# Start of a two-layer decoder trunk: loads on another queue, turns in another order, first matmul chunk in three parts, zero fills later

## The reference

```python
for i in range(2):
    x = x + 0.5 * swiglu(rmsnorm(x, ffn1_norm[i]), ffn1_w_in[i], ffn1_w_out[i])    # hidden 2816
    x = x + (s5_mixer, hgrn2_mixer)[i](rmsnorm(x, mix_norm[i]), ...)
    x = x + cross_attend(rmsnorm(x, xattn_norm[i]), mem_k[i], mem_v[i], w_q, w_o)  # 256 memory tokens
    x = x + 0.5 * swiglu(rmsnorm(x, ffn2_norm[i]), ffn2_w_in[i], ffn2_w_out[i])
y = rmsnorm(x, final_norm)
# s5: 64 groups of 16 channels, each with a 64-dim complex diagonal state
#   lam_bar = exp(lam * dt); b_bar = (lam_bar - 1) / lam * b; h_t = lam_bar * h_(t-1) + b_bar u_t
#   y_t = Re(c h_t) + d u_t, then gelu and a gated linear unit
```

## Time and profile before

| | |
|---|---|
| median of 3 runs | 2545.82 us (2538.57 to 2549.84) |
| the profiled execution | 2546.63 us |
| its span | 2544.9 us |
| PE, DVE, ACT, POOL busy | 97%, 49%, 34%, 24% of the span |
| mean granted PE clock | 0.985 |
| DMA | 289.16 MB, mean 114 GB/s |

### The profile page before, as it was taken

The page is one execution under the profiler, slowest core; times in us unless marked ns, Lnnn a source line. Parts: engine busy times, 40 slices in busy tenths (PEclk is TensorE's granted clock), DMA queues, the critical chain, the costliest instruction groups (busy, mean ns, idle before and its releaser), DMA issues.

```text
span 2544.9 us, 49720 instructions
## 1 busy us (share of the span) xinstructions
PE 2462.6 (97%) x21037; PEld 2370.9 (93%) x21037; DVE 1258.5 (49%) x1764; ACT 853.5 (34%) x1228; POOL 612.7 (24%) x604
## 2 busy tenths in 40 slices
PE   6999999799999999999999999999998999999999
PEld 6999999688976999999999999999998959999998
DVE  4553543854555543344543244466776565442443
ACT  3332221443222322222333133266664233221222
POOL 5579948241201100001211010331122203000003
PEclk8999999899999999999999999999999999999999
DMA  8255444363354333233443333333332543332332
GB/s 163 84 165 128 123 123 147 104 201 107 110 196 133 91 91 105 79 90 100 143 117 114 99 92 107 92 86 101 94 103 63 200 158 89 93 101 86 90 99 76
DMA packets 479670, 289.16 MB, mean 114 GB/s; under 512 B 22352, under 2 KB 467024, under 8 KB 478480
## 3 DMA queue, kind: packets, MB, share of 16 engines
q1 hardware_dynamic: 473760, 280.66, 37.6%
q0 software_dynamic: 848, 1.89, 0.7%
q10 hardware_dynamic: 4896, 4.20, 0.5%
HBM read 258.86 MB, written 27.85 MB: 113 GB/s over the span
## 4 chain that ended last, share of the span: by engine, by line
PE 91%; DVE 4%; ACT 2%; DMA 1%; issue 1%; POOL 1%; SPq 0%; DVEq 0%; ACTq 0%; POOLq 0%
PE lin L2670 76%; PE mis L2237 3%; DMA raw<-in_ffn_w_in_dram 1%; PE mis L2358 1%; DVE w_lo L1668 1%; DVE rstd L1681 1%; PE mis L2343 1%; PE mis L2293 1%; PE lin L2358 1%; PE mis L2523 1%; PE mis L2515 0%; PE lin L2601 0%; POOL w_lo L975 0%; DVE a_lo L1674 0%; DVE kc L1726 0%
## 5 line engine op out<-in xcount | busy, mean ns | idle before, releaser
L2670 PE MATMUL lin<-a_hi,w_hi 128*128 128x260 f32 x3584 | 1023.9, 286 | 18.9 <-DVE w_lo L1668 15.0
L2670 PE MATMUL lin<-a_lo,w_hi 128*128 128x260 f32 x3584 | 1015.8, 283 | 0.0
L2670 PE MATMUL lin<-a_hi,w_lo 128*128 128x260 f32 x3584 | 1015.2, 283 | 0.0
L2670 PEld LDWEIGHTS lin<-a_hi,w_hi 128*128 128x128 f32 x3584 | 677.1, 189 | 25.6 <-issue 12.8
L1668 DVE TENSOR_TENSOR w_lo<-raw,w_hi 128x1024 fp32r<-128x1024 f32 (+1 forms) x328 | 499.1, 1522 | 403.8 <-ACT w_hi L1239 403.4
L2670 PEld LDWEIGHTS lin<-a_hi,w_lo 128*128 128x128 f32 x3584 | 678.2, 189 | 0.0
L2670 PEld LDWEIGHTS lin<-a_lo,w_hi 128*128 128x128 f32 x3584 | 677.9, 189 | 0.2
L2670 PE MATMUL lin<-h_hi,w_hi 128*128 128x260 f32 x2016 | 570.1, 283 | 4.6 <-DVE h_lo L1898 1.7
L2670 PE MATMUL lin<-h_hi,w_lo 128*128 128x260 f32 x2016 | 569.3, 282 | 0.0
L2670 PE MATMUL lin<-h_lo,w_hi 128*128 128x260 f32 x2016 | 568.5, 282 | 0.0
L1239 ACT ACTIVATE w_hi<-raw 128x1024 fp32r<-128x1024 f32 (+1 forms) x328 | 364.5, 1111 | 320.1 <-PE lin L2670 300.0
(11 more groups left out here) (453 smaller groups left out, 2586.9 us busy)
## 6 DMA issues: line engine op xcount, KB each, us to landing
raw<-in_ffn_w_in_dram SPq DMA_DIRECT2D x176, 512.0 KB, 3.8
raw<-in_ffn_w_out_dram SPq DMA_DIRECT2D x64, 704.0 KB, 4.6
kc<-in_cache_mem_k_dram SPq DMA_DIRECT2D x32, 512.0 KB, 5.3
vc<-in_cache_mem_v_dram SPq DMA_DIRECT2D x16, 1024.0 KB, 8.6
raw<-in_hg_w_in_dram SPq DMA_DIRECT2D x32, 512.0 KB, 4.1
raw<-in_xattn_w_kv_dram SPq DMA_DIRECT2D x16, 512.0 KB, 4.3
raw<-in_s_w_glu_dram SPq DMA_DIRECT2D x16, 512.0 KB, 4.0
raw<-in_xattn_w_q_dram SPq DMA_DIRECT2D x16, 512.0 KB, 4.0
```

The source lines that it names most:

```text
L2670: ins = pe.matmul(lin[:, j, half, 0:HT], w[:, j, k, :], x[:, k, cols], start=k == 0 and u == 0, stop=k == kt - 1 and u == 2)
```

## The change

1. The nine `vrows` loads are issued by ACT, ahead of everything else it does; the memset of `vrows` is gone, and PE turns 113 rows instead of 128.
2. PE turns the prompt first, `vrows` behind it, the sample rows last. DVE copies in the same order.
3. ACT's first weight split stands behind two `a_hi` tiles instead of ahead of all.
4. The first chunk runs in three parts: all `w_hi*a_hi`, all `w_lo*a_hi`, all `w_hi*a_lo`, each waiting only for what it reads.
5. `cRaw` is loaded behind the weight loads of pair 1, `bRaw` behind those of pairs 3 and 4. The semaphore they shared is two.
6. The zero fills stand on POOL behind the state-space parameters and ahead of the wait for `mem_out`.

```diff
+            def s5_matrices(i):
+                if i == 1:
+                    for q, name in enumerate(("s5_c_re", "s5_c_im")):
+                        for e in range(2):
+                            sp.dma_start(cRaw[:, q, :, 64 * e:64 * e + 64],
+                                         i_[name][0].rearrange("(t g) c p -> (g c) t p", t=8)).then_inc(s5_cin, 16)
+                else:
+                    q = i - 3
+                    b = i_[("s5_b_re", "s5_b_im")[q]][0].rearrange("(j g) p c -> g p j c", g=2)
                     for g in range(2):
-                        sp.dma_start(bRaw[64 * g:64 * g + 64, q], b[g]).then_inc(s5_bc, 16)
...
+                        if ST[n][:2] == ("ffn1_in0", 0) and (i, j) in ((1, 1), (3, 1), (4, 1)) and s5_norm is not None:
+                            s5_matrices(i)
@@ POOL
-            step.link(pool.memset(vrows[:], 0.0))
-            for name, row in (("ffn1_norm", V_FFN1), ...):
-                pool.dma_start(vrows[row:row + 2 * KD, :], ...).then_inc(vrows_loaded, 16)
...
-            pool.wait_ge(consts_done, 4)
-            for d in range(CS - 1):
-                n = SC * (CS - 1 - d)
-                pool.dma_start(s5_t[SC * d:SC * (d + 1), :, 0:n],
-                               zeros[0:SC, 0:n].unsqueeze(1).to_broadcast([SC, SG, n]))\
-                    .then_inc(s5_zeros_out, 16)
...
                 pool.wait_ge(s5p_fill, S5P.at("c", (1, 1)) + 1)
+                pool.wait_ge(consts_done, 4)
+                for d in range(CS - 1):
+                    n = SC * (CS - 1 - d)
+                    pool.dma_start(s5_t[SC * d:SC * (d + 1), :, 0:n],
+                                   zeros[0:SC, 0:n].unsqueeze(1).to_broadcast([SC, SG, n]))\
+                        .then_inc(s5_zeros_out, 16)
                 pool.wait_ge(mem_out, 16 * 2 * DEPTH)
@@ ACT
+            for name, row in (("ffn1_norm", V_FFN1), ...):
+                act.dma_start(vrows[row:row + 2 * KD, :], ...).then_inc(vrows_loaded, 16)
...
-            split(0, 0, ST[0][3])
...
             for m in range(KD):
+                if m == 2:
+                    split(0, 0, ST[0][3])
                 gain_hi(m, NORM_ROW[0])
@@ PE
-            pe.wait_ge(vrows_loaded, 16 * 9)
-            pe.transpose(lin[:, 0, 0, 0:P], vrows[:], ident[:]).then_inc(vec_tr, 1)
             for t in range(4):
                 pe.wait_ge(rows_in[t], 16)
...
+            pe.wait_ge(vrows_loaded, 16 * 9)
+            pe.transpose(lin[:, 0, 0, 0:NVEC], vrows[0:NVEC, :], ident[0:NVEC, 0:NVEC]).then_inc(vec_tr, 1)
...
+                def first_chunk():
+                    pe.wait_ge(hi_ready, 1)
+                    for u, (w, x) in enumerate(((w_hi, x_hi), (w_lo, x_hi), (w_hi, x_lo))):
+                        if u == 1:
+                            pe.wait_ge(lo_ready, 1)
+                        for k in range(kt):
+                            if u == 0:
+                                pe.wait_ge(a_hi_done, k + 1)
+                            if u == 2:
+                                pe.wait_ge(a_lo_done, k + 1)
+                            for half in range(2):
+                                ins = pe.matmul(lin[:, 0, half, 0:HT], w[:, 0, k, :], x[:, k, half * HT:(half + 1) * HT],
+                                                start=k == 0 and u == 0, stop=k == kt - 1 and u == 2)
+                    ins.then_inc(chunk_done, 1)
+                    first_sums()
```

More of the change, by code:

```diff
@@ L372, in trunk_kernel @@
     gated = sem("gated")
-    s5_rows, s5_bc, s5_small = sem("s5_rows"), sem("s5_bc"), sem("s5_small")
+    s5_rows, s5_bin, s5_cin, s5_small = sem("s5_rows"), sem("s5_bin"), sem("s5_cin"), sem("s5_small")
     s5_sin, s5_phase, s5_square, s5_inverse = sem("s5_sin"), sem("s5_phase"), sem("s5_square"), sem("s5_inverse")
@@ L705, in s5_parameters @@
                 sp.dma_start(ldrow[64:96, :], i_["s5_log_dt"][0].rearrange("(j g) -> j g", g=2)).then_inc(s5_rows, 16)
-                for q, name in enumerate(("s5_b_re", "s5_b_im")):
-                    b = i_[name][0].rearrange("(j g) p c -> g p j c", g=2)
-                    for g in range(2):
-                        sp.dma_start(bRaw[64 * g:64 * g + 64, q], b[g]).then_inc(s5_bc, 16)
[L710 to L713, removed]
+            def s5_matrices(i):
[7 more added lines that the diff above has]
+                    b = i_[("s5_b_re", "s5_b_im")[q]][0].rearrange("(j g) p c -> g p j c", g=2)
+                    for g in range(2):
+                        sp.dma_start(bRaw[64 * g:64 * g + 64, q], b[g]).then_inc(s5_bin, 16)
             def kv_memory(l):
@@ L1083, in s5_discretize @@
                 powers(pool, link, pw, bTmp)
-                pool.wait_ge(s5_bc, 16 * 8)
+                pool.wait_ge(s5_bin, 16 * 4)
                 col = [v[q].unsqueeze(2).to_broadcast([P, NJ, SC]) for q in (6, 7)]
@@ L1249, in gain_hi @@
                                scale=vec[:, bass.ds(row + m, 1)]).then_inc(a_hi_done, 1)
+            for name, row in (("ffn1_norm", V_FFN1), ("mix_norm", V_MIX), ("xattn_norm", V_XA), ("mem_norm", V_MEM),
+                              ("ffn2_norm", V_FFN2), ("hg_lb_logits", V_LB)):
+                act.dma_start(vrows[row:row + 2 * KD, :], i_[name].rearrange("l (k p) -> (l k) p", p=P))\
+                    .then_inc(vrows_loaded, 16)
+            act.dma_start(vrows[V_FIN:V_FIN + KD, :], i_["final_norm"].rearrange("(k p) -> k p", p=P))\
+                .then_inc(vrows_loaded, 16)
+            act.dma_start(vrows[V_D:V_D + KD, :], i_["s5_d"][0].rearrange("(k g) c -> k (g c)", k=KD))\
+                .then_inc(vrows_loaded, 16)
+            act.dma_start(vrows[V_HG:V_HG + 1, :], i_["hg_norm"]).then_inc(vrows_loaded, 16)
             for t in range(4):
@@ L1681, in reciprocal @@
                 step.link(dve.reciprocal(rstd[:], t1[:]))
-            dve.wait_ge(vec_tr, 1)
-            dve.tensor_copy(vec[:], lin[:, 0, 0, 0:NVEC]).then_inc(vec_done, 1)
             for t in range(4):
@@ L1689, in _ @@
                                 mis[:, 2 * t % 4, :].rearrange("p (k t) -> p k t", k=4)).then_inc(in_evac["dve"], 1)
+            dve.wait_ge(vec_tr, 1)
+            dve.tensor_copy(vec[:], lin[:, 0, 0, 0:NVEC]).then_inc(vec_done, 1)
             dve.wait_ge(in_tr, 9)
@@ L2276, in prepare @@
                     elif what == "c":
-                        pe.wait_ge(s5_bc, 16 * 8)
+                        pe.wait_ge(s5_cin, 16 * 4)
                         e, f = a
@@ L2658, in stream @@
                     x_done, x0 = a_lo_done, KD * split_norms.index(r_in)
+                def first_chunk():
[13 more added lines that the diff above has]
+                    first_sums()
                 def chunk(p, j, first):
+                    if first and r == 0:
+                        first_chunk()
+                        return
                     pe.wait_ge(lo_ready, 2 * p + j + 1)
@@ L2672, in chunk @@
                     ins.then_inc(chunk_done, 1)
-                    if first and r == 0:
-                        first_sums()
-                    elif first and r is not None:
+                    if first and r is not None:
                         sums(r)
```

## The result

| | before | after |
|---|---|---|
| median of 20 runs each, in turn on one chip | 2545.81 us (2537.94 to 2551.33) | 2551.94 us (2544.05 to 2680.72) |
| ratio of after to before, 95% | | 1.0023 (1.0013 to 1.0033) |
| the profiled execution, its span | 2546.63, 2544.9 us | 2558.74, 2556.9 us |
| mean granted PE clock | 0.985 | 0.981 |

One run of after, that of 2680.72 us, had a granted clock of 0.85 where the others have 0.98, and the ratio leaves it out. The ratio is 5.9 us, between 3.3 and 8.4; the forecast was +3.6. So the kernel is slower, by less than the 0.5% that the prediction set as its bound. The profiled execution of after lies 6.8 us above its median (it is the slowest of the other nineteen), that of before 0.8; its stretches show where time goes, and the ratios how much it is in all.

A forecast was written before the change was run, and what follows sets the result against it. PE, busy 97% of the span, was taken as the bound. On the profiled 2546.6 us, -11.4 for the start and +15.0 for the fills gave 2550.2, forecast as 2550 us; whole range 2534 to 2559, the forecast's own 2545 to 2556.

The forecast's parts named there:

- Turns, issue of `vrows`, split: At the start: turns follow the landings, last tile done at 11.2 us; `a_hi` starts at 12.6, 7.0 us earlier.
- First chunk: At the start: only two `w_hi*a_lo` matmuls stand behind the last `a_lo`; it ends at 25.8 us, 11.7 us gained.
- Clock: At the first sums and second chunk: PE's clock may fall after idling, losing 0 to 4.2 us; taken as 1.
- Start in all: The start, with the stop at pair 1: 11.7 - 1.0 + 0.7 = 11.4 us gained, between 8 and 12.4.
- Fills, step 1: At the fills' new place on POOL: issued from 148.3 us, they fill the engines 23.9 us, until 172.2.
- stretched: Rival at the new place: fills and traffic slow each other, fills last 30 us; loss 24, time 2558 us; chance 0.09.
- Steps 2 and 3: Behind the fills: the load of chunk (10,1) takes 19 us instead of 3.8, and PE stands still 9.5 us.
- Step 4: At `ffn1_out0`: its load lands at 181.8 us; PE begins at 185.6 instead of 170.6, 15.0 us lost in all.
- Step 5: At POOL's tables: they start 16 us late and would hold PE 12.6 us, less than the 15 already lost.
- hidden: Rival at the new place: weight loads pass the fills, or fills end sooner; 2534 us, or 2533; chance 0.16.
- half: Rival at the new place: the load of chunk (10,1) takes some 12 us, not 19; 2541 to 2543 us; chance 0.15.
- The start does not follow: Rival at the start: clock stays down through the sums, or turns wait; 4 us less gain, 2554 us; no chance given.

The follow-up runs named there:

- experiment 11: The kernel before with only the zero fills spread over POOL's later tables: median 2543.51 us, ratio to before 0.9984.
- experiment 2: The kernel before with only the zero fills moved to the new place, ahead of the wait for `mem_out`: median 2560.05 us, ratio to before 1.0069.
- experiment 7: The changed kernel with the fills on ACT's hardware queue, behind the split of chunk (9,1) and ahead of the load of (10,1): one run, 2556.89 us.
- experiment 1: The changed kernel with the zero fills back in their old place behind POOL's squares: median 2538.24 us, ratio to before 0.9981.
- experiment 10: The changed kernel with fills spread over POOL's later tables, and the `vrows` loads back on POOL's queue: median 2533.93 us, ratio to before 0.9944.
- experiment 3: The changed kernel with the zero fills spread over POOL's later state-space tables: median 2531.42 us, ratio to before 0.9955.
- experiment 8: The changed kernel with fills spread over POOL's later tables, and the first chunk back in its old order: median 2537.02 us, ratio to before 0.9955.

## Why the prediction was right, and which terms were off

The forecast of 2550 us, +0.2%, holds, and its mechanism with it. By its own steps, in the profiled execution:

- **Turns, issue of `vrows`, split.** Turns began at 4.34 us (forecast 4.3). The nine issues held ACT until 5.1 us (4.2), and its first copy began at 6.40; `vrows` had landed when PE wanted it. The last tile was turned at 12.46, not 11.2. The forecast took 1.3 us a tile from the 5.12 us of the earlier trace rows, but that is a mean of two paces: 12 of those turns took 2.77 us, the other 20 only 2.35. In the profiled execution of after all 32 ran at the slow pace, 1.84 us a tile, so that the third tile, started at 8.78, still held PE when the fourth had landed (at about 10.1, forecast 9.9). That is the 1.0 us by which `a_hi` is late. The granted clock reads 1.00 in both stretches, so no row says why the pace differs. In the eight other runs with the new start and `vrows` on ACT the pace rose earlier, and PE came to `vrows` at 9.61 to 11.13 us (forecast 11.2).
- **First chunk.** Ended at 27.4 us (25.8). DVE's string took 12.2 us (12.0), and with the 1.0 us it ended 1.1 late; the last matmuls behind it ran at the lower clock (0.50 in the window from 26 us).
- **Clock.** Taken as 1 us: the sums took 4.76 instead of 3.67, so it was right in after; in the run with spread fills the window from 26 to 30 us was at 1.00, and nothing was lost. Both were within the bounds. The sums lost 1.1 to 1.7 us in three of the ten profiled executions with the new start, and nothing in seven.
- **Pair 1.** The stop of 0.7 us is gone, as forecast. By experiment 11 the early fills cost more than their stop, 4.1 us (1.3 to 7.1); the forecast had nothing for that.
- **Start in all.** 10.2 us against 11.4, bounds 8 to 12.4. Together with spread fills it is worth 11.4 us by the ratio, alone 7.4 by ratios and 11.7 by marks (experiment 11).
- **Matrices.** Nothing, as forecast, and the run with them in their old place agrees.
- **Fills, step 1.** Forecast to last 23.9 us; they lasted 28, most of the way to the 30 of the "stretched" rival. In the old place they took 24.1 us. Whether the traffic of q1 stretches them is open: beside the same loads and stores they took 25.4 us in experiment 2. The 0.36 us a packet of the prediction mixes the 288 packets of `vrows` in; the 560 of the fills, 73.9% of the engines from 29 to 54 us before, are 0.53 us each. The forecast of 23.9 us did not rest on it.
- **Steps 2 and 3.** The load took 20.6 us (19), the first stop was 11.0 (9.5).
- **Step 4.** The second load landed at 173.8 us. The forecast, 181.8, is 171.6 in these times. `ffn1_out0` began 6.9 us later than before; with the 10.2 of the start, 17.1 us were lost there, against 15.0.
- **What the step left out.** I had counted the lower clock after the stop for chunk (10,1), where the second stop hides it, but not after the second stop: from 177.41 to the mark are 10.7 us, before 8.1. That is 2.6 us more. It stood only in the "stretched" rival.
- **Step 5.** POOL's tables were 18 us late in shifted times (16), and PE did not wait for them. The run with the parking stores moved shows how near they were.

So the term that was mis-sized is the cost of the fills: 15.0 us forecast, 19.7 by the trace of after, 17.6 (13.5 to 21.4) with the fills moved alone, 17.3 (12 to 22) between after and spread fills. The start was 1.2 us too high. Both errors have the same sign, so they did not cancel; the sum came out as +3.6 against +5.9 (3.3 to 8.4). The prediction also held that a change under 0.5% could not be told from none. With 20 runs each, 0.23% could: the interval does not reach 1.

The rivals: "hidden" and "half" are out, by the 20.6 us of the load. "Stretched" was right that PE meets `ffn1_out0` at the lower clock; its 30 us of fills were not reached (28.0), and the weight load had landed 3.3 us before the last fill. "The start does not follow" is out.

The place of the fills was the whole question, and a rule of the Trainium skill ("DMA: Bandwidth & Descriptors", the section on queues, rings and completion order) bore on it: an engine drains a whole packet of one queue, of typically 9 to 17 descriptors, before it turns to the next. The trace agrees: 7168 rows in 560 packets are 12.8 rows each, and with one row a packet the load beside them took 8.4 us, not 20.6 (with the reserve made at experiment 7). The fit in the same page's section on the anatomy of one DMA, an estimate of 6.2 us for 1.8 MB taken as one transfer, comes near the long rows (8 us from the first issue to the last landing) and is wrong for the short ones (28 us), so there the measurement decides.

## What to carry to other kernels

A transfer that nobody waits for still needs a place: ask which load will stand behind it and how much cover that load's user has there. Here many short rows, issued at once on POOL's queue, delayed the loads behind them by most of their own duration; one at a time they cost nothing that showed. And after a stop of PE of several microseconds, as the two here, add the slower microseconds behind it to the price, at every stop that another doesn't hide.

## What the runs showed of the hardware that was not expected

- On a hardware queue the same short rows move the cost to the issuer: ACT was held for 19.5 us by seven issues that take POOL 5.6 us. SP, whose issue of a store is 0.34 us, took 3.17 us in after and 2.98 in experiment 2 for a store with the delayed weight load ahead of it on q1, and 15.72 us in experiment 1 for the two loads of `cRaw` that took 1.64 in after.
- The time of the fills hardly depends on the queue: 23.9 to 28.0 us from first issue to last landing on POOL's (the five runs that issue them at once, before included), 22.7 and 25.0 on ACT's.
- Profiled executions of one kernel lie up to 11 us above its median (2544.88 against 2533.93 in experiment 10), and there most of it arises behind the mark, which stands only 3.1 us later than in experiment 3. A gain of 3.6 us at the mark (experiment 8) need not be found in a ratio of this width.
